# Mixing the turns of x and h2 with the early U chunks, eleven chunks at the head

## The reference, cut to what matters

```
h  = rmsnorm(x) * (1 + scale1) + shift1;  x += gate1 * (mixer(h) @ W_out)
h2 = rmsnorm(x) * (1 + scale2) + shift2
q  = h2 @ W_query;  scores = q . sub_keys      # 8 heads, 2 halves, 128 keys each
top 16 of each half -> 16x16 sums -> top 16    # (row, column) of 128 x 128 experts
gates = softmax(best)
act  = gelu(h2 . expert_u[idx]);  x += gate2 * sum(gates * act * expert_v[idx])
y  = rmsnorm(x)
```

## Time and profile before

| | |
|---|---|
| median of 3 runs | 2042.55 us |
| lowest, highest | 2037.83, 2048.38 us |
| span of the profiled execution | 2047.7 us |
| PE busy | 1925.9 us (94%) |
| DVE busy | 1532.2 us (75%) |
| ACT busy | 837.2 us (41%) |
| POOL busy | 736.2 us (36%) |
| mean granted TensorE clock | 0.975 |

### The profile page before, as it was taken

How to read it: one execution, slowest core, us unless ns; L and a number is a source line. 1 busy time by engine, 2 the same in 40 slices (tenths; PEclk the granted TensorE clock), 3 DMA queues, 4 the chain that set the end, 5 groups by cost and what they waited for, 6 DMA issues and landing times.

```text
span 2047.7 us, 33886 instructions
## 1 busy us (share of the span) xinstructions
PE 1925.9 (94%) x12849; PEld 1740.7 (85%) x12849; DVE 1532.2 (75%) x3001; ACT 837.2 (41%) x1439; POOL 736.2 (36%) x571
## 2 busy tenths in 40 slices
PE   5999999999859899888889999999999999999997
PEld 3789999999748799788889889889898988898986
DVE  4476666666544578789986697878888888888888
ACT  3334344334222323579993333333333333333333
POOL 0010000000031233488981344444444545545463
PEclk8999999999879999899999999999999999999999
DMA  8712222222033222637668999999999999999974
GB/s 348 313 58 78 78 68 78 68 68 78 32 136 124 83 73 80 231 113 235 194 201 296 352 341 364 345 337 334 352 357 328 353 344 344 346 350 341 353 278 146
DMA packets 171663, 460.81 MB, mean 225 GB/s; under 512 B 15728, under 2 KB 72400, under 8 KB 168176
## 3 DMA queue, kind: packets, MB, share of 16 engines
q1 hardware_dynamic: 125424, 290.87, 40.3%
q0 software_dynamic: 46080, 167.79, 22.1%
HBM read 416.98 MB, written 41.62 MB: 224 GB/s over the span
## 4 chain that ended last, share of the span: by engine, by line
PE 55%; DVE 6%; POOL 2%; DMA 2%; issue 1%; ACT 1%; another core or an unknown queue 0%; DVEq 0%; SPq 0%; ACTq 0%
PE pp L2211 20%; PE dd L2224 17%; PE pp L2224 8%; PE pp L426 5%; PE pp L1880 3%; POOL hot_a L2018 2%; DVE hot_b L2440 1%; PE dd L2179 1%; DMA v_raw<-in_v 1%; DVE hot_a L2444 1%; PE dd L2134 1%; DMA gate_matrix<-gstage 1%; DVE w_lo L414 0%; DVE cand L2523 0%; DVE cand L2528 0%
## 5 line engine op out<-in xcount | busy, mean ns | idle before, releaser
L426 PE MATMUL pp<-act_hi,w_hi 128*128 128x272 f32 x1216 | 281.9, 314 | 19.8 <-DVE act_lo L1835 6.6
L410 ACT ACTIVATE w_hi<-w_raw 128x1024 fp32r<-128x1024 f32 x204 | 214.7, 1052 | 191.0 <-PE pp L426 145.7
L2211 PE MATMUL pp<-act_hi,w_hi 128*128 128x384 f32 x792 | 268.6, 339 | 1.7 <-DVE acc L2675 1.7
L2211 PE MATMUL pp<-act_lo,w_hi 128*128 128x384 f32 x792 | 266.9, 337 | 0.0
L2211 PE MATMUL pp<-act_hi,w_lo 128*128 128x384 f32 x792 | 266.2, 336 | 0.0
L426 PE MATMUL pp<-act_lo,w_hi 128*128 128x272 f32 x1216 | 254.8, 291 | 0.0
L426 PE MATMUL pp<-act_hi,w_lo 128*128 128x272 f32 x1216 | 254.7, 291 | 0.0
L414 DVE TENSOR_TENSOR w_lo<-w_raw,w_hi 128x1024 fp32r<-128x1024 f32 x178 | 219.3, 1232 | 29.7 <-ACT w_hi L410 29.6
L426 PEld LDWEIGHTS pp<-act_hi,w_hi 128*128 128x128 f32 x1216 | 193.6, 193 | 38.6 <-issue 17.1
L2377 ACT ACTIVATE co_hi<-cf 128x384 fp32r<-128x384 f32 x128 | 67.5, 527 | 348.6 <-PE pp L2224 308.0
L426 PEld LDWEIGHTS pp<-act_lo,w_hi 128*128 128x128 f32 x1216 | 195.4, 193 | 0.0
(11 more groups left out here) (378 smaller groups left out, 4134.2 us busy)
## 6 DMA issues: line engine op xcount, KB each, us to landing
w_raw<-in_stream SPq DMA_DIRECT2D x204, 512.0 KB
v_raw<-in_v SPq DMA_DIRECT2D x128, 512.0 KB
ada_w<-in_ada SPq DMA_DIRECT2D x24, 1024.0 KB, 11.6
gt<-gate_matrix SPq DMA_DIRECT2D x31, 768.0 KB
gate_matrix<-gstage SPq DMA_DIRECT2D x11, 2048.0 KB, 9.9
early<-cst SPq DMA_DIRECT2D x28, 192.0 KB, 3.9
cst<-early SPq DMA_DIRECT2D x28, 192.0 KB
s_s<-in_delta SPq DMA_DIRECT2D x8, 512.0 KB, 7.2
```

Of the source, the lines that this page charges most:

```text
L410: nc.scalar.activation(w_hi[k.slot][:], w_raw[k.slot][:], ACT.Copy).then_inc(w_hi_done, 1)
L426: last = nc.tensor.matmul(pp[s][:, b, 0:HN], w[:, c * P:(c + 1) * P], a[:, c, b * HN:(b + 1) * HN], start=(c == 0 and w is w_hi[s] and a i ...
L2211: last = nc.tensor.matmul(pp[s][:, 0, 0:TD], w[:, c * P:(c + 1) * P], a[:, c, 0:TD], start=(c == 0 and w is w_hi[s] and a is act_hi), stop ...
```

## The change: what it does

The ten turns are cut into halves, and PE runs half an early chunk ahead of each half turn. Ten early chunks and ten turns go together; the eleventh early chunk stands behind `turn(0)`. `E_HEAD` is 11 and not 10, so 17 and not 18 chunks are left for the quads. ACT takes each half turn out of its bank around the `early_gelu` of its chunk, and repeats h2 and the gate in the first four rounds; `exponents(0)` and `exponents(1)` stand in the rounds 3 and 7. POOL issues its first eight fetches in pairs behind the `w_lo` of chunks 6, 7, 8 and 9. SP stores each turn behind its chunk's load and store.

```diff
-        E_QUERY, E_HEAD, LOW_LAG = 4, 10, 5
+        E_QUERY, E_HEAD, LOW_LAG = 4, 11, 5
...
# POOL
-                pool.wait_ge(chosen, 1)
-                pool.wait_ge(turned, 2 * TT)
-                for n in range(RING):
-                    fetch(pool, n)
                 for i in range(E_QUERY, E_HEAD):
                     early_low(pool, Chunk(C_EARLY + i + 2))
+                    for n in range(2 * (i - E_QUERY), min(2 * (i - E_QUERY) + 2, RING)):
+                        if n == 0:
+                            pool.wait_ge(chosen, 1)
+                            pool.wait_ge(turned, 2 * TT)
+                        fetch(pool, n)
...
# SP
+                for i in range(E_HEAD):
+                    load_chunk(sp, Chunk(C_EARLY + i + 4))
+                    store_early(sp, i)
+                    if i < len(TURNS):
+                        store_turned(i)
...
# PE (turn_half is the body of the loop over the halves, as before)
-                early_pieces(pe, (E_HEAD - E_QUERY) * KC)
+                for i in range(len(TURNS)):
+                    for half in range(2):
+                        early_pieces(pe, KC // 2)
+                        turn_half(i, half)
+                turn(0)
+                early_pieces(pe, KC)
                 pe.wait_ge(turned_out, 2 * len(TURNS))
-                turn(0)
...
# ACT
+                for i in range(E_HEAD):
+                    if i < len(TURNS):
+                        turn_out(i, 0)
+                    early_gelu(act, i)
+                    if i < len(TURNS):
+                        turn_out(i, 1)
+                    for k in range(2 * i, 2 * i + 2):
+                        if k < KC:
+                            repeat(k)
+                    if i == 3:
+                        exponents(0)
+                    elif i == 7:
+                        exponents(1)
```

More of the change, by code:

```diff
@@ L2030, in _, with store_turned @@
                     load_chunk(sp, Chunk(C_QUERY + k))
[L2031 to L2035, removed]
+                def store_turned(n):
+                    kind, t = TURNS[n]
                     if kind == "own":
-                        continue
+                        return
                     sp.wait_ge(turned_out, 2 * n + 2)
@@ L2045, in store_gates @@
                                      gates_st[b % 2], 16)
-                for i in range(E_QUERY, E_HEAD):
-                    load_chunk(sp, Chunk(C_EARLY + i + 4))
-                    store_early(sp, i)
                 for q in range(n_quads):
@@ L2143, in _ @@
                 score(2 * H - 1)
[L2144 to L2169, removed]
@@ new lines, in turn_half @@
+                def turn_half(n, half):
+                    kind, t = TURNS[n]
+                    if n == 0 and half == 0:
+                        pe.wait_ge(sc_read, 2 * H + 2)
+                    if 2 * n + half >= 3:
+                        pe.wait_ge(turned_out, 2 * n + half - 2)
+                    bank = banks[(2 * n + half) % 3]
+                    for q in range(4):
+                        k = 4 * half + q
+                        at = slice(q * P, (q + 1) * P)
+                        if kind == "x":
+                            rows = P if t < NC else TS
+                            last = nc.tensor.transpose(bank[0:rows, at], x[:, k, t * P:t * P + rows], ident)
+                        elif kind == "row":
+                            pe.wait_ge(repeated, 2 * KC)
+                            g = ((mod[:, G2 + k, 0:1].to_broadcast([P, P]), P), (g2_rep[:, k, :], TS),
+                                 (v_("gf")[:, k:k + 1].to_broadcast([P, P]), P))[t]
+                            last = nc.tensor.matmul(bank[0:g[1], at], g[0], ident, start=True, stop=True)
+                        elif t == 0:
+                            pe.wait_ge(h2_whole, KC)
+                            last = nc.tensor.transpose(bank[:, at], h2[:, k, SPARSE_P * P:(SPARSE_P + 1) * P], ident)
+                        else:
+                            last = nc.tensor.transpose(bank[:, at], h2_rep[:, k, :], ident)
+                    last.then_inc(turned, 1)
@@ L2191, in turn @@
                     last.then_inc(picks_tr, 1)
[L2193 removed]
+                assert len(TURNS) == E_HEAD - 1
+                for i in range(len(TURNS)):
[4 more added lines that the diff above has]
+                early_pieces(pe, KC)
                 pe.wait_ge(turned_out, 2 * len(TURNS))
[L2195 removed]
                 for u in range(ND):
@@ L2273, in _ @@
                 keep(2 * H - 1)
-                for i in range(E_QUERY):
-                    early_gelu(act, i)
                 act.sem_inc(quad_read, 4)
@@ L2284, in exponents, with repeat @@
                     nc.scalar.activation(of, of, ACT.Exp).then_inc(ex_out, 1)
-                for k in range(KC):
+                def repeat(k):
                     nc.scalar.activation(h2_rep[:, k, :].rearrange("p (r t) -> p r t", r=NRQ),
@@ L2292, in _, with turn_out @@
                                          ACT.Copy).then_inc(repeated, 1)
-                for n, (kind, t) in enumerate(TURNS):
+                def turn_out(n, half):
+                    kind, t = TURNS[n]
                     rows = TS if (kind, t) in (("x", NC), ("row", 1)) else P
-                    if kind != "own" and n >= 4:
+                    if kind != "own" and n >= 4 and half == 0:
                         act.wait_ge(turn_st[n % 4], 16 * (n // 4))
                     to = own_of[t] if kind == "own" else turn_sb[n % 4]
[L2298 to L2302, removed]
+                    act.wait_ge(turned, 2 * n + half + 1)
+                    nc.scalar.activation(to[0:rows, half * 512:(half + 1) * 512], banks[(2 * n + half) % 3][0:rows],
+                                         ACT.Copy).then_inc(turned_out, 1)
+                for i in range(E_HEAD):
[8 more added lines that the diff above has]
+                    if i == 3:
                         exponents(0)
+                    elif i == 7:
+                        exponents(1)
                 aways = [0]
@@ L2339, in store_row @@
                                          ACT.Copy).then_inc(quad_read, 1)
[L2341 to L2344, removed]
                 for s in range(4):
```

## The result

| | before | after |
|---|---|---|
| median of 22 runs | 2040.38 us | 2045.99 us |
| lowest, highest | 2033.61, 2048.38 | 2042.06, 2053.94 |
| ratio after to before | | 1.0027, 95% interval 1.0019 to 1.0036 |
| span of the profiled execution | 2047.7 us | 2045.8 us |

The changed kernel is 5.6 us slower; the forecast was 4 us faster. The two profiles say the reverse of the runs: the span after is 1.9 us shorter. That contradiction is the case. A profiled execution's device time is 1.8 us over its span (2047.58 for 2045.8), so the profile of before was of an execution at about 2049.5, 9 us above the median of 22 runs and above the slowest of them (2048.38): it isn't one of the 22. Everything in the prediction was measured from it.

What follows compares the result with a forecast made beforehand. PE was taken to bound the head until turn(0), then DVE; beyond PE's gain DVE's two choices set the end. -3.4 (DVE's lead) - 1.25 (one w_lo fewer) + 0.6 (POOL) = -4 us from the median: 2038 us, range 2022 to 2049.

Steps and rivals of the forecast that it cites:

- end of the first choice: In the head, DVE's choice(0), delayed by w_lo on POOL, has chosen ready at 838.1 instead of 834.10.
- end of the picks: In the head, DVE's choice(1) ends at 869.3, 2.4 us later than before, and sets turn(0).
- first quad's end: Behind turn(0), the cold eleventh chunk delays ACT's and POOL's hots, so the first quad ends at 883.7.
- fifth hot step: In DVE's quads, this step would come at 880.8 but is held to 883.8, leaving DVE 3.4 us ahead.
- at chunk 7: In the head, PE is ready for chunk 7 at 841.0 and waits 2.1 us for its w_lo from POOL.
- The meetings of DVE and POOL: In the choices, some DVE instructions stand still while POOL subtracts w_lo; 12.7 us taken, between none and 19.6.
- I take the -4 from the median: Final sum: -4 us, worked out against the 2047.7 us span, applied to the median 5.1 us lower, giving 2038.
- DVE's wait of 9.38 us: Ahead of turn(0), DVE's wait after choice(1) is all that a faster PE can take from DVE as it stands.
- DVE isn't last: Rival at turn(0): meetings few or short, turn(0) at 856.5, gain 19.3 + 1.25, 2022 us; chance 0.25.
- The quads go by POOL: Rival in the quads: POOL's columns start at 880.5 and its 13.7 us idle stays, 2043 us; chance 0.15.
- DVE's choices are held longer: Slower rival in the head: all meetings whole plus 4.1 us of pauses, picks at 880.3, 2049 us; chance 0.15.
- The dense pass: The dense pass keeps its length; the prediction is wrong if it changes by over 3 us.

Runs made afterwards that it cites:

- small_lo: Changed kernel with POOL computing only 8 columns of w_lo for early chunks from 4 on, the rest left stale; 2028.5 us beside 2047.7 for the kernel before.
- before_fourth: The kernel before, unedited, profiled a fourth time on another chip; 2041.1 us beside 2041.5 for the kernel before.
- the first set: The original comparison, 22 runs each of the kernel before and the changed kernel; 2040.4 and 2046.0 us.
- set C: A later set on one chip, with the changed kernel unedited and variants beside the kernel before; changed kernel 2044.7 us, kernel before 2039.9.
- before_again: The kernel before, unedited, run again for a second profile; 2047.4 us beside 2047.7 for the kernel before.
- after_again: The changed kernel, unedited, run again; 2045.7 us beside 2047.7 for the kernel before.
- set A: The first set of follow-up experiments, on one chip, both kernels unedited and variants; kernel before 2047.7 us, changed kernel 2045.7.
- ahead: Changed kernel with the eleventh chunk ahead of turn(0) instead of behind it; 2038.7 us in both sets, beside 2047.7 and 2039.9 for the kernel before.
- mixed_ten: Changed kernel with ten chunks at the head and nothing behind turn(0), 18 chunks left for the quads; 2039.7 us beside 2047.6 for the kernel before.
- before_eleven: The kernel before with an eleventh early chunk behind turn(0), nothing else changed; 2046.5 us beside 2047.6 for the kernel before.

## Why the prediction was wrong

**Each step on the changed kernel held, within 2 us.** In the prediction's positions, less 804.2: end of the first choice 33.9, measured 33.6; end of the picks 65.1, measured 64.3 to 66.2 in four profiles; PE ready at 54.5, measured 55.4; idle 10.6, measured 8.9 to 10.8; first quad's end 14.4 us behind turn(0), measured 14.3 (874.31 to 888.64); fifth hot step 79.6, measured 79.2 to 80.6. One piece was wrong without consequence: at chunk 7 PE waited 0.23 us for POOL and not 2.1, because the halves of the row turns have eight instructions each and take 1.05 us and not 0.47. The meetings of DVE and POOL, bounded between 0 and 19.6 us and taken at 12.7, cost about 12 by small_lo; that the total came out this close is in part luck, since a shift of 0.2 us can move the picks by some 2 us.

**The step that failed is the other side of the subtraction:** "I take the -4 from the median". The 5.1 us between the profiled span and the median were taken for a spread that both kernels share. The larger part of the 9 us between that execution and the 22 runs were, as far as before_fourth can stand for those runs, the 3.01 and 3.65 us pauses themselves. Those are not in every execution of the kernel before: without them turn(0) stands at 63.0, not at 71.4, and the fifth hot step at 74.4, not at 83.1. Against that the changed kernel's 79.2 to 80.6 is 4.8 to 6.2 us later; less the 1.25 us of one w_lo that is 3.6 to 5.0, where 5.6 was measured in the first set and 4.8 in set C. Against before_again, with the pauses (fifth hot step 80.4), after_again is 1.2 us earlier, with the 1.25 2.4 faster, where 2.0 was measured in set A. One mechanism gives both signs.

The same mistake stands in the first paragraph: DVE's wait of 9.38 us was called what a faster PE can take. In an execution without pauses it is 0.81 (take(0) in before_fourth), and the mixing has nothing to take. What is left of the change is its costs: 1.5 to 3.3 us of picks, from more w_lo beside the choices, and 6.6 from turn(0) to the first quad (12.3 for 5.7), of which DVE's four steps of lead hide half.

**The rivals.** "DVE isn't last" fell: DVE was last at turn(0) in every profile of the changed kernel and its variants but small_lo. "The quads go by POOL": POOL's idle there stayed at 12.6 us, but ahead and mixed_ten moved the end by moving the first quad, so POOL doesn't set it. "DVE's choices are held longer" had the sign and not the cause: the picks were where the forecast had them. The dense pass kept its length, as expected: from the first to the last start of its V products it took 952.3 us in the first profile after and 952.6 in the one before.

**The best version** is ahead: 2038.7 us in both of its sets, 6 to 7 less than the changed kernel; against the kernel before 0.9955 beside its upper level and 1.0000 beside its lower one. Where there are no pauses, then, nothing of the change is a gain. mixed_ten is within 1 us of it.

## What to carry to other kernels

Before an idle time of the profile is counted as gain, ask whether it is in the median: compare the profiled execution's device time with the runs, and take a second profile when it stands at their edge. A chunk of work that goes behind a hand-over can hold up every queue behind it (12.3 us to the first quad); ahead of the hand-over, in the idle time, the same chunk left turn(0) where it was (64.4). Work moved to POOL beside DVE's two-input operations is not free for DVE: eight subtractions cost it about 12 us in small_lo, 1.5 each, where DVE does one itself in 1.25. And a forecast of such meetings is good to some 2 us only (picks at 64.0 and at 65.9 in one program), since 0.2 us decide what falls on what.

## What the runs showed of the hardware

- ACT and PE paused for 2.0 to 3.7 us at a time, in the same place of three profiles of the kernel before and of before_eleven, and not at all in before_fourth, with the same program. What they waited for was done: the semaphores rose late (3.07 us from PE's last product to ACT's copy, 0.04 in before_fourth). By this, it seems, one kernel on one core has two levels, 7 us apart, that differ between sets on different chips.
- DVE's scalar operations, copies and two-input operations stood still for the rest of a POOL subtraction (0.22 became 2.77 us, 1.83 became 4.03), reductions and index searches did not (1.81 and 0.22 beneath one). Where a DVE product was 0.15 us ahead, the pair kept its 1.83 us and POOL's subtraction took 3.31 instead of 2.40.
- 10.8 us without work put TensorE at 1.2 GHz (clock 0.50); turn(0) then took 1.11 (0.63 in before_fourth, behind 0.20 us of idle).
